# Last rows by a 0/1 product, z1 taken k-tile by k-tile, and mask rows inside the score product

## The reference

```python
for l in range(DEPTH):                              # 2
    h = rmsnorm(x, norm_mix[l])
    z = h @ w_in[l]                                 # 512 x 1440
    aq, ak, av, bq, bkv, bkr = split(z)
    oa = swa_sink_attention(aq, ak, av, positions, sinks[l])      # 8 heads of 64, window of 2 chunks of 64
    qb = rmsnorm(bq, q_norm[l]) @ w_qb[l]           # 8 heads of 64 + 32 (rotary)
    kvb = rmsnorm(bkv, kv_norm[l]) @ w_kvb[l]
    ob = mla_attention(qn, qr, kn, kr, vb)          # s = q.k; masked where key_chunk > q_chunk; softmax
    gates = sigmoid(h @ w_gate[l] + b_gate[l])
    x = x + (ga * (oa @ w_oa[l]) + gb * (ob @ w_ob[l])) @ w_out[l]
    h = rmsnorm(x, norm_ffn[l])
    x = x + hierarchical_moe(h, ...)                # top-1 of 8 groups, top-2 of its 8 experts, SwiGLU of 256
return rmsnorm(x, norm_final)
```

## Time and the profile before

| | us |
|---|---|
| median of 3 runs | 2032.73 (2031.26 to 2032.86) |
| profiled execution | 2034.93 |
| its span, first to last instruction | 2033.3 |
| PE busy | 1943.7 |
| DVE busy | 1412.0 |
| ACT busy | 1205.7 |
| POOL busy | 158.5 |
| mean granted TensorE clock | 0.978 |

### The profile page before, as it was taken

How to read it: one execution, slowest core, us unless ns; L and a number is a source line. 1 busy time by engine, 2 the same in 40 slices (tenths; PEclk the granted TensorE clock), 3 DMA queues, 4 the chain that set the end, 5 groups by cost and what they waited for, 6 DMA issues and landing times.

```text
span 2033.3 us, 27015 instructions
## 1 busy us (share of the span) xinstructions
PE 1943.7 (96%) x9266; PEld 1578.2 (78%) x9266; DVE 1412.0 (69%) x1792; ACT 1205.7 (59%) x1512; POOL 158.5 (8%) x175
## 2 busy tenths in 40 slices
PE   8999999999999999999689999999999999999994
PEld 6977777788888888888579777777888888888883
DVE  4454443568999899899544544435689998999895
ACT  4444443337777777777444544433477777777773
POOL 0000000021110111011000000000301100110010
PEclk9999999999999999999889999999999999999997
DMA  4253113559999999999421711134799999999992
GB/s 148 82 133 97 42 42 110 196 182 387 383 369 374 381 382 368 379 380 376 152 111 53 175 56 42 42 130 176 256 386 388 376 364 381 389 366 366 386 355 90
DMA packets 157960, 500.66 MB, mean 246 GB/s; under 512 B 22288, under 2 KB 38672, under 8 KB 157872
## 3 DMA queue, kind: packets, MB, share of 16 engines
q1 hardware_dynamic: 146192, 459.70, 61.3%
q0 software_dynamic: 11680, 39.80, 6.4%
HBM read 486.79 MB, written 29.63 MB: 254 GB/s over the span
## 4 chain that ended last, share of the span: by engine, by line
PE 93%; DVE 3%; ACT 2%; issue 1%; DMA 1%; POOL 0%; POOLq 0%; DVEq 0%; ACTq 0%; SPq 0%
PE ps L1453 27%; PE ps L1455 26%; PE ps L1454 26%; PE ps L1677 3%; PE ps L1606 2%; PE ps L1610 2%; PE ps L1663 1%; PE ps L1807 1%; DVE wl L1015 1%; PE ps L1768 1%; PE ps L1722 1%; PE ps L1501 1%; PE ps L1780 1%; DMA y<-yrows 1%; PE ps L1496 0%
## 5 line engine op out<-in xcount | busy, mean ns | idle before, releaser
L1015 DVE TENSOR_TENSOR wl<-raw,wh 128x2048 fp32r<-128x2048 f32 (+1 forms) x402 | 907.4, 2279 | 188.5 <-ACT wh L666 185.9
L666 ACT ACTIVATE wh<-raw 128x2048 fp32r<-128x2048 f32 (+1 forms) x406 | 753.8, 1883 | 76.6 <-PE ps L1455 68.3
L1453 PE MATMUL ps<-wh,xgh 128*128 128x512 f32 x1024 | 414.8, 405 | 0.0
L1455 PE MATMUL ps<-wh,xgl 128*128 128x512 f32 x1024 | 402.9, 393 | 0.0
L1454 PE MATMUL ps<-wl,xgh 128*128 128x512 f32 x1024 | 401.8, 392 | 0.0
L1455 PEld LDWEIGHTS ps<-wh,xgl 128*128 128x128 f32 x1024 | 192.6, 188 | 43.6
L1454 PEld LDWEIGHTS ps<-wl,xgh 128*128 128x128 f32 x1024 | 193.1, 189 | 37.8
L1453 PEld LDWEIGHTS ps<-wh,xgh 128*128 128x128 f32 x1024 | 192.8, 188 | 37.9
L1453 PE MATMUL ps<-wh,hth 128*128 128x512 f32 x512 | 200.9, 392 | 2.0 <-DVE htl L1038 2.0
L1454 PE MATMUL ps<-wl,hth 128*128 128x512 f32 x512 | 200.7, 392 | 0.0
L1455 PE MATMUL ps<-wh,htl 128*128 128x512 f32 x512 | 200.7, 392 | 0.0
(11 more groups left out here) (295 smaller groups left out, 2613.0 us busy)
## 6 DMA issues: line engine op xcount, KB each, us to landing
raw<-in_w SPq DMA_DIRECT2D x512, 512.0 KB, 6.0
raw<-in_w SPq DMA_DIRECT2D x128, 1024.0 KB
raw<-in_w_gate SPq DMA_DIRECT2D x16, 1024.0 KB
xslots<-zrow POOLq DMA_DIRECT2D x2, 6240.0 KB, 35.2
xg<-xslots POOLq DMA_DIRECT2D x16, 520.0 KB, 7.2
raw<-in_w_out SPq DMA_DIRECT2D x8, 1024.0 KB
raw<-in_w_in SPq DMA_DIRECT2D x8, 800.0 KB
raw<-in_w_oa SPq DMA_DIRECT2D x4, 1024.0 KB
```

The lines of the kernel that those rows point to most:

```text
L666: return nc.scalar.activation(dst, src, ACT.Copy)
L1015: return V.tensor_tensor(dst, src, hi.bitcast(F32), ALU.subtract)
L1453: MM(dst, lh, rh, start=first, stop=False)
L1455: return MM(dst, ll, rh, start=False, stop=last)
```

## The change

It has three parts.

1. z1. The first units are split k-tile by k-tile (`first_high`, `first_low`), between the pieces of h1, and the product runs k-tile by k-tile over all five groups. The turned halves go to other banks, first halves of all tiles ahead of second halves of tiles 1 to 3. The warm-up products of layer 0 are five instead of eight. Before layer 1 only k-tile 0 is split ahead of the squares.
2. Masks. `mask_rows` is made by POOL at the start and stored to HBM. In each layer POOL loads four rows of it into the rows 96 to 99 of the turned queries and keys of every head. The score product runs over 100 rows, and the separate product of one row is gone.
3. Last rows. Blocks 0 to 6 are stored by index as before, into yrows, which POOL now sets to zero first. In block 7 POOL loads yrows to yb tile by tile and DVE adds each tile to x (`earlier_rows`). Also in block 7 DVE makes a 0/1 matrix from the place of every token in the last group (`selection`), PE turns it, and ACT copies it. When block 7 ends, ACT and DVE split its y into yh and yl (`y_high`, `y_low`), PE multiplies them by the 0/1 matrix tile by tile (`y_product`), and DVE adds the products to x (`add_half`). An overflow block is treated like block 7. `y_product` of block 7 stands ahead of PE's overflow loop.

```diff
+        def chained_blocks(eng, body, leave, give=None):
             def more(b, _):
-                if leave:
-                    leave(b - 1)
+                leave(b - 1)
                 body(FIRST + LAST, ND, b, b, prepared=False, prepare=False)
+                if give:
+                    give(b)
...
             body(NEXT + LAST, ND + len(FIRST), NG - 2, NG - 1, prepared=True, prepare=False)
+            if give:
+                give(NG - 1)
             return overflow(eng, more)
...
+                for i, at in enumerate((qt, kt)):
+                    pool.dma_start(at[QD:QD + NT, :, :], masks[i].rearrange("r (o c) -> r o c", o=1)
+                                   .to_broadcast([NT, HEADS, T])).then_inc(S["pool_in"], 16)
                 pool.wait_ge(S["kt_ev"], 2 * NT)
                 pool.dma_start(xslots[l], zrow[0].partition_broadcast(SLOTS)).then_inc(S["zero_in"], 16)
+                pool.dma_start(yrows, zrow[0, 0:D].partition_broadcast(T)).then_inc(S["zero_in"], 16)
...
-                n_blocks = blocks(pool, move_block)
+                with pool.Fori(0, NG - 1) as b:
+                    move_block(b, b)
                 for t in range(NT):
-                    pool.dma_start(y8[:, t, :], tiles(yrows)[:, t]).then_inc(S[f"y8_in{t}"], 16)
+                    if t:
+                        pool.wait_ge(S["xm_done"], t)
+                    pool.dma_start(yb[:, :], tiles(yrows)[:, t]).then_inc(S["y8_in"], 16)
...
+            def y_high(b):
+                act.wait_ge(S["used_m"], b * NU + NU)
+                for h in range(2):
+                    nc.scalar.activation(yh[:, h * 512:(h + 1) * 512], ps[5 + h][:, :], ACT.Copy
+                                         ).then_inc(S["yh_done"], 1)
...
+            def y_low(b):
+                for h in range(2):
+                    dve.wait_ge(S["yh_done"], (b - (NG - 1)) * 2 + (h + 1))
+                    cols = slice(h * 512, (h + 1) * 512)
+                    V.tensor_tensor(yl[:, cols], ps[5 + h][:, :], yh[:, cols].bitcast(F32), ALU.subtract
+                                    ).then_inc(S["yl_done"], 1)
+
+            def add_half(b, t, h):
+                if (t, h) == (0, 0):
+                    dve.wait_ge(S["xm_done"], NT)
+                    dve.wait_ge(S["x8_done"], (b - (NG - 1)) * NT + BASE["x8_done"])
+                dve.wait_ge(S["yp_ps"], (b - (NG - 1)) * 2 * NT + (2 * t + h + 1))
+                cols = slice(h * 512, (h + 1) * 512)
+                last = V.tensor_tensor(xl[:, t, cols], xl[:, t, cols], ps[4 * h + t][:, :], ALU.add)
...
+                        if u == ("up", 2, 0) and not prepare:
+                            selection()
+                        if kind == "up" and 3 <= e < 3 + NT and half == 0 and prepared and not prepare:
+                            earlier_rows(e - 3)
...
+                for k in range(KD):
+                    n = first_unit(k)
+                    pe.wait_ge(S["lk_done"], k + 1)
+                    if k == 0:
+                        pe.wait_ge(S["h1l_done"], NT + 1)
+                    if k == KD // 2:
+                        pe.wait_ge(S["h1l_done"], 2 * NT)
+                    for m in range(AH // 2 + 1):
+                        last = mm3(ps[m][:, :], *part(n, k, m * P, P), h1h[:, k, :], h1l[:, k, :], k == 0, k == KD - 1)
...
-                        MM(dst[:, 0:n], qt[0:QD, h, tok], kt[0:QD, h, 0:n], start=True, stop=True)
-
-                        last = MM(dst[:, n - CHUNK:n], rowsel[:, :], negrow[:, :], start=False, stop=True,
-                                  skip_group_check=True)
+                        rows = slice(0, QD + NT)
+                        last = MM(dst[:, 0:n], qt[rows, h, tok], kt[rows, h, 0:n], start=True, stop=True)
...
+                        if u == ("up", 3, 0) and not prepare:
+                            pe.wait_ge(S["sel_made"], (b - (NG - 2)) * NT)
+                            for t in range(NT):
+                                last = nc.tensor.transpose(ps[7][:, t * P:(t + 1) * P], sel[:, t, :], ident[:, :])
+                            last.then_inc(S["selt_ps"], 1)
+
+                def y_product(b):
+                    pe.wait_ge(S["selt_done"], b - (NG - 2))
+                    if isinstance(b, int):
+                        stay_awake(8)
+                    for t in range(NT):
+                        tok = slice(t * P, (t + 1) * P)
+                        for h in range(2):
+                            cols = slice(h * 512, (h + 1) * 512)
+                            if t == 0:
+                                pe.wait_ge(S["yl_done"], (b - (NG - 1)) * 2 + (h + 1))
+                            MM(ps[4 * h + t][:, :], selt[:, tok], yh[:, cols], start=True, stop=False)
+                            MM(ps[4 * h + t][:, :], selt[:, tok], yl[:, cols], start=False, stop=True
+                               ).then_inc(S["yp_ps"], 1)
```

More of the change, by code:

```diff
@@ L369, in pieces, with first_unit, first_pieces @@
             return got
+        def first_unit(k):
+            return next(n for n in range(*U_Z1) if plan[n][1] <= k < plan[n][1] + plan[n][2])
+        def first_pieces(k, at, as_loaded=False):
+            n = first_unit(k)
+            return pieces(n, at, as_loaded)[2 * (k - plan[n][1]):2 * (k - plan[n][1]) + 2]
         def product_ready(eng, signal, m, groups, units):
@@ L683, in _ @@
             for l in range(L):
-                done = [1 if l else 0]
+                done = [U_Z1[1]]
                 def split_to(n):
@@ L716, in root, with turned_high @@
                                          ).then_inc(S["diag_done"], 1)
[L718 to L723 removed]
+                def turned_high(t, c):
+                    act.wait_ge(S["h1_ps"], 2 * t + c + 1)
+                    nc.scalar.activation(h1h[:, 4 * c:4 * c + 4, t * P:(t + 1) * P],
+                                         ps[4 * c + t][:, :].rearrange("p (k q) -> p k q", k=4), ACT.Copy
+                                         ).then_inc(S["h1h_done"], 1)
+                if l:
+                    first_high(0)
                 square(0)
@@ L729, in _ @@
                 root(1)
-                turned_high(0)
-                square(3)
-                root(2)
-                turned_high(1)
-                root(3)
-                turned_high(2)
-                split_to(1)
-                turned_high(3)
+                if l == 0:
+                    square(3)
+                    root(2)
+                turned_high(0, 0)
+                if l:
+                    square(3)
+                    root(2)
+                turned_high(0, 1)
+                root(3)
+                turned_high(1, 0)
+                turned_high(2, 0)
+                if l == 0:
+                    first_high(0)
+                turned_high(3, 0)
+                first_high(1)
+                first_high(2)
+                for t in range(1, NT):
+                    turned_high(t, 1)
+                for k in range(3, KD):
+                    first_high(k)
                 split_to(U_Z1[1] + 1)
@@ L1040, in _ @@
             for l in range(L):
-                done, steps = [1 if l else 0], [0]
+                done, steps = [U_Z1[1]], [0]
                 def split_to(n):
@@ L1473, in part, with columns_product @@
                     return hi_at(n)[:, o:o + cols], lo_at(n)[:, o:o + cols]
-                def columns_product(units, groups, act_h, act_l, signal, cols_of, free=None, ready=None):
+                def columns_product(units, groups, act_h, act_l, signal, cols_of, free=None):
                     first_k, last_k = plan[units[0]][1], plan[units[1] - 1][1] + plan[units[1] - 1][2] - 1
@@ L1494, in _ @@
                     pe.wait_ge(ident_in, 1)
-                    for _ in range(8):
+                    for _ in range(5):
                         MM(ps[7][:, :], ident[:, :], ident[:, :].rearrange("p (o q) -> p o q", o=1)
```

266 lines of the change are left out of this document (168 added, 98 removed).

## The result

| | before | after |
|---|---|---|
| median, same chip | 2032.36 (4 runs) | 2008.41 (4 runs, 2007.76 to 2011.58) |
| ratio | | 0.9887, 95% 0.9874 to 0.9899 |
| profiled execution | 2034.93 | 2008.32 |
| its span | 2033.3 | 2006.4 |

What follows compares the result with a forecast made beforehand. TensorE bounds the kernel, with 93% of the chain of waits. 10.6 + 5.4 - 1.6 + 9.5 + 17.1 = 41.0 takes the profiled 2034.93 to 1993.9; the runs' median is 2.2 lower, so 1991.7, range 1986 to 2003.

Steps and rivals of the forecast that it cites:

- The zeroing of yrows: On POOL's queue, 2 MB longer under lightly loading gates; nothing waits for it until routing: cost 0.
- The mask rows: Attention, both layers: dropping the mask product saves 0.085 x 32 per layer, 5.4 us; bounds 0 and 7.7.
- Between the layers: Last down product to layer 1's z1: z1 starts at 1016.9 instead of 1034.01, gain 17.1 us; bounds 12.5 to 18.2.
- the rival with 13%: Between the layers, PE's overflow loop takes longer: hole 4.3 us, clock falls, turning and z1 slower; 1998.4; chance 13%.
- The start: Layer 0 up to z2: z2 starts at 43.2, gain 10.6 us; bounds 5 to 11.5.
- block 7: Last rows inside block 7: added PE and DVE work loses 0.8 us a layer, 1.6 us together.
- the end: After the last expert product: first output row starts at 2015.3 instead of 2024.78, gain 9.5 us; bounds 7.5 to 9.8.
- z1's order: Layer 0: z1 needs only k-tile 0 and the first four k-tiles of h1, starting at 15.9 instead of 24.67.
- late read-backs: Block 7: read-backs landing in 9.5 us make DVE 5 us past its margin, 10 in both layers; 2002; chance 12%.
- a first stage held by weights: Layer 0's first stage, held by weights or ACT's order, gets half of its gain; 1997; chance 8%.
- mask rows without effect: Attention: the mask rows bring nothing; 1997; chance 5%.
- a slower kernel: Block 7 loses more than 20.5 us a layer to very late read-backs; some 2035 at 15 us landing; chance 3%.

Runs made afterwards that it cites:

- early zeroing: The changed kernel with the zeroing of yrows issued right behind the mask loads, some 33 us earlier; 1981.10, ratio to before 0.9743.
- both repairs: Mask product over 128 rows, against the kernel before: 2021.65; window keys zero-padded to 128 rows, against the changed kernel with yrows zeroed earlier and PE's loop behind a test: 1959.83.

## Why the prediction was wrong

**The zeroing of yrows, costed at nothing: this step failed, and it is the largest.** The text said "under gates that load DMA lightly, and nothing waits for it until routing: 0". It asked who waits for the zeroing and not who stands behind its bytes. "Lightly" was read from a mean: the DMA share is 0.28 over the 190 us of the earlier trace rows, but before the change it was already full for part of them, while the slots were zeroed:

```profile
140.00:160.00 20.00, 20.00 (x101) 15.75 (x101) 8.50 (x36) 10.18 (x34) 0.00 (x0) 1.00 1.00 209
```

Into that stretch went 2 MB more. The load of 1 MB that was asked for 18 us after the zeros, 8.3 MB by now, took 28.76 us. What is late next is ACT's split of the gate's weights, then everything in ACT's order behind it, then PE: 11.14 - 2.59 = 8.55 us in one step of layer 0 and 5.32 - 3.18 = 2.14 in the next, where the clock was down. Price: 10 to 12 us a layer (early zeroing: attention 12.2 and 10.0 shorter). Before, with the zeroing of the slots alone, PE was busy for all of the 20 us above. Shown by one moved line.

**The mask rows: the mechanism was right, the term mis-sized.** 5.4 was forecast and 20.5 measured, with the bound at 7.7. The step that failed is "A score product of 256 columns without a mask product holds PE for 191.92 - 191.30 = 0.62; with it, 194.75 - 194.04 = 0.71", together with "rows cost nothing visible here: 64-row and 96-row products fit one line". The line was drawn through two products that both paid for few rows. A 96-row score without a mask product behind it, the case that was wanted, is in no row of before: when it was made, the product behind it started 191.25 - 190.95 = 0.30 after it, and the MLA step came out 0.15 shorter than the window step of the same columns. 0.32 is 0.11 for the product and 0.21 for loads that are not hidden under or behind a product of one row; the window score pays 0.34 for its 64 rows.

These two nearly cancel (22 lost, 20.5 won), and a reading of the total, or of attention alone, would have found neither. It was luck that the total missed by no more than 17 us: the mask rows brought 15.1 more than forecast and hid most of what the zeroing lost.

**Between the layers: the rival with 13% was right.** Forecast: hole 2.0, turning 7.2, z1 15.8 after the last down product; measured 5.68, 9.88 and 22.1. The failed step is "the overflow loop to pass, which takes ACT 2.30": ACT's row held (2.30 again) and PE's price is another. PE's loop skips larger bodies; that their size is the reason was not tested. One skip alone leaves a hole of 3.50, none 0.86. The hole that was forecast for that rival, 4.3, was still too short. The sign that the text had named for this, a wait by issue of over 3 us ahead of the turning, was there. The rule that spoke for it (Trainium skill, Runtime: NRT & Kernel Launch, Instruction fetch mechanics: a taken branch out of the fetched pages must fetch its target first) agrees in so far as a packet of instructions stands in the hole with branches and none without; that packet takes 0.97 of the 5.68 us. So the branches are shown to be the cause, and what else they wait for is open. The clock followed as that rival had it: PE's last product ended at 999.4, the clock was at 1.00 until 1003 and at 0.50 from 1004. The 1.8 us that the rival set down for a slow z1 did not come: z1 took 27.3 us. Without the loop everything else of this step held: 14.8 us.

**The start** was 0.85 off, by warm-ups that lasted until 8.6 and not "near 7.1". In the trace before, ten warm-up matmuls, as many as five products make, are through at 7.5, and there the granted clock rose at 4.6; after the change it rose at 6.8. This differs from one profile to the next. In six other traces with the old start it rose at 6.5 to 7.7 and z2 started at 55.2 to 56.0, and in the six with the new one z2 starts at 43.5 to 44.5. So this part is worth some 11.5 us, and the pair of profiles shows 9.75 because the one before was a good one.

**Right:** block 7 (+1.1 for +1.6; reads in time, DVE without a wait, selections 0.87 for about 1, transposes 0.60 for 0.55), the end (-9.6 for -9.5), z1's order. The rivals of late read-backs, of a first stage held by weights, of mask rows without effect and of a slower kernel were all wrong.

The sum by measured terms: 9.75 + 20.5 - 22.2 - 1.1 + 10.9 + 9.6 = 27.45, against 26.9 in the spans; of the difference, 0.3 lies in the stretches outside the table.

## What to carry to other kernels

Ask of a transfer that nobody waits for which transfers stand behind its bytes, over the whole time that it takes to land and with its neighbours' bytes added; put bulk zeroing where no weights are asked for. A price read as the difference of two rows is only as good as the row taken as "without": look at the weight loads (does one start ahead of its product or with it?) before calling a product cheap. A loop that does nothing has a price, on each engine another (2.30 us idle on ACT, 5.68 on PE), and it is paid where that engine is just about to be needed. Read a DMA share over the stretch that matters, and not as a mean over a stage.

## What was not expected of the hardware

Among products of 96, 100 and 128 rows, each weight load ran under the product ahead of it. At a change from such a product to one of 1 or 64 rows, or back, the load started only with its own product, after an idle time of up to 0.33 us: this costs 0.21 and 0.34 us a product. Few rows alone don't stop a load: the two loads of a window score, both of 64 rows, are over at 191.59, and its two matmuls last until 192.00. So it may be the change in rows that is dear, and not the small product; both repairs took away the small products and the changes together, so no run tells the two apart. Making a product larger, from 1 row to 128 or from 64 to 128, made the kernel faster by 11.4 and 16.9 us. Whether the limit lies at 64 rows or between 64 and 96 was not tried.

A branch around a block's body on PE: the hole is 0.86 us with none (and that is ACT's), 3.40 to 4.03 in the three versions with one, 5.62 and 5.68 in the two with three. The first makes the hole some 2.5 to 3.2 longer, each further one 0.8 to 1.1.

With nothing to do, PE kept its clock for 3.2 us before the change and for 4.1 us after it, and lost it both times; in a hole of 0.86 us (without the loop) it kept it. With one branch it had already resumed after 3.50 us, and the clock still fell, 4.5 us after its last product.
